# Values as weights and weighted transposition in the compressed-key attention layers of a four-layer transformer kernel

## What is computed

```
gates = sigmoid(g_logit)                       # one per head and branch
s_c = q . ck * scale - slope * dist_c ; p_cmp = masked_softmax(s_c)
o_cmp = p_cmp @ cv                             # 31 compressed keys
s_s = q . k_sel * scale - slope * dist ; o_sel = masked_softmax(s_s) @ v_sel
s_w = q . k_win * scale - slope * dist ; o_win = masked_softmax(s_w) @ v_win
out = g0 * o_cmp + g1 * o_sel + g2 * o_win
return out @ w_out
```

## Time and profile before

| | us |
|---|---|
| median of 3 runs | 2615.0 (2614.6 to 2615.92) |
| the profiled execution | 2615.86 |
| its span, first to last instruction | 2614.1 |
| TensorE busy | 2551.6 (98%) |
| VectorE busy | 1630.7 (62%) |
| ScalarE busy | 1171.1 (45%) |
| GpSimd busy | 359.3 (14%) |

### The profile page before, as it was taken

The page is one execution under the profiler, slowest core; times in us unless marked ns, Lnnn a source line. Parts: engine busy times, 40 slices in busy tenths (PEclk is TensorE's granted clock), DMA queues, the critical chain, the costliest instruction groups (busy, mean ns, idle before and its releaser), DMA issues.

```text
span 2614.1 us, 38319 instructions
## 1 busy us (share of the span) xinstructions
PE 2551.6 (98%) x13432; PEld 2152.9 (82%) x13432; DVE 1630.7 (62%) x2821; ACT 1171.1 (45%) x1799; POOL 359.3 (14%) x322
## 2 busy tenths in 40 slices
PE   8999999999999999999999999999999999999997
PEld 6999978888878677888878878888779998788886
DVE  6588667664252847667256676673386885766733
ACT  4367544443232845444235554443343774544421
POOL 2011121110010522111010021110010111211100
PEclk9999999999999999999999999999999999999999
DMA  4410023333233022332321123333333001233231
GB/s 156 142 33 1 26 81 97 96 96 98 81 109 97 17 65 89 97 96 90 106 79 62 41 81 103 96 97 97 94 113 105 9 2 49 89 97 97 88 105 48
DMA packets 61907, 210.90 MB, mean 81 GB/s; under 512 B 8528, under 2 KB 10320, under 8 KB 61776
## 3 DMA queue, kind: packets, MB, share of 16 engines
q1 hardware_dynamic: 61776, 209.13, 26.0%
HBM read 207.01 MB, written 2.10 MB: 80 GB/s over the span
## 4 chain that ended last, share of the span: by engine, by line
PE 90%; DVE 7%; ACT 1%; issue 1%; POOL 0%; DMA 0%; SPq 0%; DVEq 0%; ACTq 0%; POOLq 0%
PE psum L304 21%; PE psum L306 21%; PE psum L305 21%; PE psum L1077 6%; PE psum L1065 3%; PE psum L906 3%; PE psum L908 3%; PE psum L907 3%; PE psum L1055 2%; PE psum L1054 2%; DVE xl L477 2%; DVE h L494 2%; PE psum L338 1%; DVE dh L493 1%; PE psum L332 1%
## 5 line engine op out<-in xcount | busy, mean ns | idle before, releaser
L304 PE MATMUL psum<-xh,w_hi 128*128 128x512 f32 x1712 | 667.0, 390 | 0.1
L305 PE MATMUL psum<-xh,w_lo 128*128 128x512 f32 x1712 | 666.1, 389 | 0.0
L306 PE MATMUL psum<-xl,w_hi 128*128 128x512 f32 x1712 | 666.1, 389 | 0.0
L266 DVE TENSOR_TENSOR w_lo<-w_raw,w_hi 128x1024 fp32r<-128x1024 f32 x226 | 280.3, 1252 | 513.5 <-ACT w_hi L260 511.2
L260 ACT ACTIVATE w_hi<-w_raw 128x1024 fp32r<-128x1024 f32 x226 | 236.2, 1057 | 564.9 <-PE psum L306 455.1
L304 PEld LDWEIGHTS psum<-xh,w_hi 128*128 128x128 f32 x1712 | 321.4, 188 | 66.8 <-issue 0.6
L306 PEld LDWEIGHTS psum<-xl,w_hi 128*128 128x128 f32 x1712 | 321.3, 188 | 66.8
L305 PEld LDWEIGHTS psum<-xh,w_lo 128*128 128x128 f32 x1712 | 321.4, 188 | 66.4
L698 DVE TENSOR_TENSOR w_lo<-w_raw,w_hi 128x1024 fp32r<-128x1024 f32 x160 | 209.3, 1308 | 253.7 <-ACT w_hi L694 253.7
L304 PE MATMUL psum<-ah,w_hi 128*128 (+1 forms) x704 | 273.9, 389 | 0.0
L305 PE MATMUL psum<-ah,w_lo 128*128 (+1 forms) x704 | 273.9, 389 | 0.0
(11 more groups left out here) (198 smaller groups left out, 3837.4 us busy)
## 6 DMA issues: line engine op xcount, KB each, us to landing
w_raw<-w_up SPq DMA_DIRECT2D x176, 512.0 KB, 3.6
w_raw<-w_down SPq DMA_DIRECT2D x88, 512.0 KB, 3.6
w_raw<-nsa_in SPq DMA_DIRECT2D x56, 512.0 KB, 3.7
w_raw<-sb_in SPq DMA_DIRECT2D x24, 512.0 KB, 3.7
w_raw<-nsa_out SPq DMA_DIRECT2D x16, 512.0 KB, 3.7
w_raw<-swa_in SPq DMA_DIRECT2D x10, 512.0 KB, 3.7
w_raw<-sb_out SPq DMA_DIRECT2D x8, 512.0 KB, 3.7
w_raw<-swa_out SPq DMA_DIRECT2D x8, 512.0 KB, 3.7
```

The source lines that it names most:

```text
L266: nc.vector.tensor_tensor(w_lo[:, u % RING, :], w_raw[:, u % RING, :], w_hi[:, u % RING, :].bitcast(F32), ALU.subtract).then_inc(split_don ...
L304: nc.tensor.matmul(bank(p, o), wh[:, k, o, :], xhi(k), start=(first and k == 0), stop=False)
L305: nc.tensor.matmul(bank(p, o), wl[:, k, o, :], xhi(k), start=False, stop=False)
L306: mm = nc.tensor.matmul(bank(p, o), wh[:, k, o, :], xlo(k), start=False, stop=(last and k == 1))
```

## The change

In the two compressed-key layers the attention is written anew (`pe_steps`, `dve_steps`, `act_steps`, `pool_steps`); the sliding-window layer keeps the old functions. The unit is a step: two heads (a = 0, 1) and one query block, 16 steps per group, 64 per layer, in the order group, branch b, pair of heads p, i = 3, 2, 1, 0.

- Row sums come from the exponentials (`accum_out` into `rsums`). GpSimd takes the maximum with 1e-30 (`floor`), VectorE the reciprocal (`weights`), GpSimd multiplies it with the gate and the result with the identity: a tile with a head's factors on its diagonal (`scaled`).
- `transposes` is a float32 product of the raw exponentials as weights with that tile, so that transposed scores come out divided and gated.
- `copy` takes two PSUM banks to `pt`, ScalarE one and VectorE the other: for i = 3 and 2 a head each, for i = 1 ScalarE takes both heads, for i = 0 VectorE.
- `values` has 64 columns of values as weights and 128 queries moving, the two heads in the two halves of the columns. Both branches and the compressed branch add up in PSUM: one product of 512 columns with the compressed values (`cvb`) opens each pair. `mixed`, `output`, GpSimd's additions, `ot` and the 32 output transpositions fall away in these layers; the result is already turned, and ScalarE and VectorE make its high and low part from PSUM (`output`, `low`), mostly during the attention.
- Order: the scores of step t + 3 stand ahead of the transposing products of step t, and the values of t - 1 behind them.

```diff
-            for g in range(G):
-                shares = (pt[:, i, :] if i < 2 else late_pt[:, i - 2, :])[:, g * P:(g + 1) * P]
-                mm = nc.tensor.matmul(mix_bank(p0, i, g // 2)[:, 256 * (g % 2):256 * (g % 2) + 256], shares,
-                                      cvb[:, g, :], start=True, stop=True, skip_group_check=True)
...
+        def pe_steps(pe, l, last_unit):
...
+            def transposes(t):
+                it, b, p, i = step_of(t)
+                pe.wait_ge(nd_done, B + t + 1)
+                if t:
+                    pe.wait_ge(nca_done, C3 + act_copies(t - 1))
+                    pe.wait_ge(ncd_done, C3 + dve_copies(t - 1))
+                for a in range(2):
+                    x, at_ = turned_at(t, a)
+                    for j in range(i + 1):
+                        mm = nc.tensor.matmul(psum[:, half_of(l, 4 + x), at_ + j * P:at_ + (j + 1) * P], raw_scores(t, a)[:, j * P:(j + 1) * P],
+                                              scaled_unit(t)[:, a, :], start=True, stop=True, skip_group_check=True)
+                    mm.then_inc(nt_done, 1)
+            def values(t):
+                it, b, p, i = step_of(t)
+                o = half_of(l, 6 + p)
+                if b == 0 and i == TC - 1:
...
+                    nc.tensor.matmul(psum[:, o, :], cvb[:, it, P * p:P * p + P], ct[:, it, :], start=True, stop=False, skip_group_check=True)
...
+                for j in range(i + 1):
+                    for a in range(2):
+                        x, at_ = turned_at(t, a)
+                        mm = nc.tensor.matmul(psum[DH * a:DH * a + DH, o, i * P:(i + 1) * P], vt[b][:, j, it, 0:DH],
+                                              pt[:, 2 * (t % 2) + x, at_ + j * P:at_ + (j + 1) * P], start=False, stop=(b == 1 and j == i),
+                                              skip_group_check=True)
...
+            last_unit(ahead)
+            scores(2)
+            for t in range(STEPS):
+                if t + 3 < STEPS:
+                    scores(t + 3)
+                transposes(t)
+                if t:
+                    values(t - 1)
+            values(STEPS - 1)
+        def act_steps(act, l, window_values):
...
+            def exps(t):
+                n = (step_of(t)[3] + 1) * P
+                for a in range(2):
+                    c = 2 * (t % 4) + a
+                    v = raw_scores(t, a)[:, 0:n]
+                    act.wait_ge(nb_done, 2 * (B + t) + a + 1)
+                    nc.scalar.activation(v, v, ACT.Exp, scale=-1.0, bias=mins[:, c:c + 1], accum_out=rsums[:, c:c + 1]).then_inc(ne_done, 1)
+            def copy(t):
+                i = step_of(t)[3]
+                n = (i + 1) * P if i >= 2 else 2 * (i + 1) * P
+                act.wait_ge(nt_done, 2 * (B + t) + (1 if i >= 2 else 2))
+                if t >= 2:
+                    act.wait_ge(nv_done, B + t - 1)
+                nc.scalar.activation(pt[:, 2 * (t % 2), 0:n], psum[:, half_of(l, 4), 0:n], ACT.Copy).then_inc(nca_done, 1)
...
+            for t in range(STEPS):
+                it, x = t // 16, t % 16
+                if step_of(t)[3]:
+                    copy(t)
+                if t + 2 < STEPS:
+                    exps(t + 2)
...
+        def dve_steps(dve, ch, l, window_keys):
...
+            for t in range(STEPS):
+                it, x = t // 16, t % 16
+                if t + 1 < STEPS:
+                    weights(t + 1)
+                if step_of(t)[3] != 1:
+                    copy(t)
+                if t + 3 < STEPS:
+                    biased(t + 3)
...
+        def pool_steps(pool, l):
...
+            def floor(t):
+                c = 2 * (t % 4)
+                pool.wait_ge(ne_done, 2 * (B + t) + 2)
+                nc.gpsimd.tensor_scalar(rsums[:, 8 + c:10 + c], rsums[:, c:c + 2], 1e-30, None, ALU.max).then_inc(nf_done, 1)
+            def scaled(t):
+                it, b, p, i = step_of(t)
+                c, x = 2 * (t % 4), 3 * (R * it + 2 * p) + 1 + b
+                pool.wait_ge(nw_done, B + t + 1)
+                nc.gpsimd.tensor_tensor(rsums[:, 24 + c:26 + c], rsums[:, 16 + c:18 + c], gat[:, i, x:x + 4:3], ALU.mult).then_inc(ng_done, 1)
+                if t >= 4:
+                    pool.wait_ge(nt_done, 2 * (B + t - 4) + 2)
+                pool.wait_ge(ng_done, B + t + 1)
+                nc.gpsimd.tensor_tensor(scaled_unit(t), ident[:].unsqueeze(1).to_broadcast([P, 2, P]),
+                                        rsums[:, 24 + c:26 + c].unsqueeze(2).to_broadcast([P, 2, P]), ALU.mult).then_inc(nd_done, 1)
...
+            floor(0)
+            for t in range(STEPS):
+                if t + 1 < STEPS:
+                    floor(t + 1)
+                scaled(t)
...
```

More of the change, by code:

```diff
@@ L1146, in output @@
                         sums = bk[:, :, DH:DH + 1].rearrange("p t o -> p (t o)")
[L1147 to L1151, removed]
+                        dve.wait_ge(es_done, it * (n // 4) + (job + 1))
+                        mark[0] = ch.then(nc.vector.tensor_tensor(rs, sums, esink[:, job % 2, :], ALU.add))
                     if 1 in steps:
@@ L1186, in turn @@
                         output(job, (2,))
[L1187 to L1195, removed]
+                    r = s // 4 + 2
+                    if s % 4 == 1 and (more or r < R):
+                        queries(it + r // R, r % R)
                 if not more:
@@ L1218, in ahead @@
                     biased(0, s)
[L1219 to L1224, removed]
+            heads_loop(dve, ahead, turn, late)
         def act_attention(act, l, kind, late=None):
@@ L1260, in turn @@
                     exps(s)
-                    if kind == "nsa" and it == 0 and s == 1:
-                        late()
                     if 1 <= s % 4 <= 2:
                         copy(s - 1)
[L1265 to L1279, removed]
+                    r = s // 4 + 2
+                    if s % 4 == 0 and (more or r < R):
+                        queries(it + r // R, r % R)
             def ahead():
-                for r in range(R if kind == "nsa" else 2):
-                    queries(0, r)
-            heads_loop(act, ahead, turn, late if kind == "swa" else None)
+                queries(0, 0)
+                queries(0, 1)
+            heads_loop(act, ahead, turn, late)
         def slope(head):
@@ L1292, in esink_bias @@
             return sinks[:, bass.ds(it * R + r, 1)]
[L1294 to L1304, removed]
[L1305 to L1314 removed]
+        STEPS = 4 * H
@@ L1554, in exps @@
                 nc.scalar.activation(v, v, ACT.Exp, scale=-1.0).then_inc(ce_done, 1)
-            def mixed(i):
-                act.wait_ge(co_done, TC * k + i + 1)
-                for q in range(2):
-                    m = ch.then(nc.scalar.activation(ot[:, i, 512 * q:512 * q + 512], mix_bank(p0, i, q), ACT.Copy))
-                act.wait_ge(s_chain, m)
-                act.sem_inc(co_ready, 1)
             exps(0)
```

272 lines of the change are left out of this document (185 added, 87 removed).

## The result

| | before | after |
|---|---|---|
| median of the runs shown, us | 2615.46 (4 runs) | 2816.49 (4 runs) |
| lowest to highest, us | 2614.6 to 2615.99 | 2815.16 to 2817.88 |
| profiled execution, us (span, clock) | 2615.86 (2614.1, 0.997) | 2815.16 (2813.4, 0.975) |

The ratio is 1.0769, 95% interval 1.075 to 1.0788: slower, by 201 us. The forecast was 2734 us with a range up to 2780: right in sign, 82 us short, and outside the range.

The account below looks back on a forecast made before the run. TensorE bounds the kernel before; afterwards a ring of waits through ScalarE and GpSimd makes a pair 13.08 us against 8.97, +59.3 per layer. Two layers add 118.6 to 2615.9: 2734 us, range 2687 to 2780.

Parts of the forecast that it names:

- TensorE's own work: Compressed-key attention: TensorE alone needs 10.76 us per pair of heads in one branch, against 8.97 before.
- rival 2: Attention stage: TensorE decides, not the wait between engines; 10.76 us per pair, 2660 us; chance 0.10.
- The ring: Attention steps: products, copy, exponentials, floor, gate, scaled identity wait in a circle; 3.71 us in i = 3, 4.15 in i = 1.
- Value passes: Value products on TensorE: 0.055 us per pass, plus 0.15 per change of array form; 3.4 us per pair against 4.2.
- a transposing pass: Transposing fp32 products on TensorE: two passes each at 0.11 us, 4.4 us per pair, 2.2 more than before.
- rival 4: Transposing products: a true fp32 product costs four times a transposition; 17.0 us per pair, 2859 us; chance 0.02.
- Rival 1: GpSimd's scaled-identity tail slows by 1.4 beside VectorE; 14.03 us per pair, 2765 us; chance 0.12.
- granted clock of 1.00: TensorE in the attention stages: 2.4 GHz as in the earlier trace; a fall would lengthen the time, no size given.
- upper bound of 2778: Whole kernel, with small GpSimd operations at 0.41 us and sums at 0.08 per exponential: 14.43 us per pair.
- the tail: GpSimd's floor, gate and scaled identity with hand-overs, behind the exponentials: 1.15 us per step.
- read of ScalarE's accumulator: ScalarE delivering sums with exponentials: 0.04 us each, 0.08 in a step; bounds 0 and 0.08 per exponential.
- changes of form for free: TensorE's array-form switches without drain cost: 0.6 us per pair falls away, time about 2715 us.

Follow-up runs that it names:

- e8: e1 plus ScalarE's exponentials of two steps on issued ahead of the copy of the step's transposed half: 2671.12 us.
- e1: Changed kernel with GpSimd forming a step's scaled identity ahead of the next step's floor, not behind it: 2692.63 us.
- e2: Changed kernel, order kept, with 16 extra overwritten score products ahead of the real ones of each i=1 step: 2779.56 us.
- e9: e2 with the exponentials' sums left out, GpSimd taking score minima instead and the output's division omitted: 2752.94 us.
- e7: e8 with the exponentials and scaled identity written as float32r, so transposing products are not fp32 products: 2599.26 us.

## Why the prediction was right in sign and 82 us short

**Right.** TensorE's own work: 10.76 us per pair was forecast, and e8, where nothing else bounds, took 174.3 us for the stage, (174.3 + 3) / 16 = 11.1. As a time of the whole this is what rival 2 says, 2660 us; e8 measured 2671. The ring was right too, in its place and its members: the wait of 1.94 us before i = 0 (forecast about 2), 0.60 before i = 2 (forecast 0.5), none before i = 3 and i = 1 that mattered, the floor waiting for the exponentials; and e1, which only breaks that order, took it away. Value passes: 16 in 1.09 us with the group behind them 1.02 on, as forecast from the earlier trace rows; a transposing pass 0.11, as read from the earlier trace rows, so rival 4 is out. Rival 1 is out too: the scaled identity took 0.61 us in all 128 cases, with VectorE at work beside it (at 259.12) and without (at 267.34). Outside the stages 7 us were given back, 7 forecast; 1.2 of them come from the start, where nothing was forecast.

**Wrong, first: the clock.** The step that failed is the one sentence under "How the numbers follow": the granted clock of 1.00 was carried over from the earlier trace rows, a stage without a gap, to a stage into which the same text put a gap of 1.8 us 16 times. That it would then be "longer still" was said, but given neither a price nor a place in the range. Its price by e2 is 37 us (2816.5 to 2779.6): in the half-clock stretches a transposing pass takes about 0.2 us, twice the 0.11 of the rows. An estimate from the stretches alone: 27 of them (two follow the last wait of a stage, of 1.73 us) last 117 us together in the trace after, so they lose at most half of that, 58 us. Put on the forecast of 2734, such a term gives 2792 us, still short of the measured time; put on the upper bound of 2778 it would have held it. The Trainium skill, TensorE: Matmul & The Clock Gate, Part 1, says that the halved clock is the default state and that activity releases it. e2 agrees: with activity in the wait the clock stays up.

**Wrong, second: the ring's small terms.** e2 has the ring at full clock: 2779.6 us, 45 over the forecast. By steps, from the first transposing product of one to that of the next, in the period of e2 from 250.71 to 264.97 us, which has no compressed values; the last row is what is missing to the mean of 14 periods, 14.46 us:

| step | forecast | measured | what was mis-sized |
|---|---|---|---|
| i = 3 | 3.71 | 4.09 | ring |
| i = 2 | 3.21 | 3.60 | ring, which was to lie under TensorE's own 3.21 |
| i = 1 | 4.15 | 4.58 | ring |
| i = 0 | 1.58 | 1.99 | products start anew behind a wait, the scaled identity of i = 3 is ready late |
| compressed values, mean | 0.43 | 0.20 | partly in the shadow of the ring |

Together 1.38 us per pair, times 32 some 44 of the 45 us. In the rows of the i = 1 step above the 0.43 divides so: the eight passes and the way to the copy 1.19 (263.43 to 264.62) against 1.08; the exponentials with their reads 1.51 (265.12 to 266.63) against 1.42; the tail behind them 1.38 (266.63 to 268.01) against 1.15. GpSimd's three operations were well sized, 0.21 + 0.20 + 0.61 against 0.18 + 0.18 + 0.64; their hand-overs were not: 0.08 + 0.08 + 0.14 + 0.06 where 0.15 stood for all. The read of ScalarE's accumulator had no row before and was put at 0.04 per exponential by VectorE's 0.08; it is an instruction of 0.19 with some 0.1 of its own on ScalarE when an exponential follows, and all of it counts when GpSimd waits. By e9 the reads cost 0.83 per pair; 0.24 was charged. The upper bound, 0.08 per read, was taken from another engine's row, and was no bound.

One sum in the prediction is off as well. With changes of form for free it takes 0.6 us per pair off the forecast and gets 2715 us. The 0.6 holds only beside its bound with GpSimd's small operations at nothing. With its own 3.16 for the ring of i = 2 the step goes from 3.21 to 3.16 only, and what falls away is some 0.5 us, 2719 us.

**Where the time went**, from before to after: TensorE's own new work 55 us (e8); ScalarE's copy ahead of the exponentials 21.5 (e8 to e1); the ring 87 (e1 to e2); the clock 37 (e2 to after). The sum is 201. These are steps along one path; the second pass, 72 us by e7 against e8, lies in the first of them, so without it TensorE's new work would have been a gain of 17.

## What to carry to other kernels

A floor of two numbers on an engine that is 16% busy can set the period of the kernel: for each engine write down which instruction stands ahead of the one that is waited for, and what that one waits for. When a forecast puts a wait on TensorE, price the clock with it, from the granted clock that the passes behind the wait would have; a wait that can't be removed may be worth filling with work that is thrown away. And before weighting inside a transposition, ask for the format: in fp32 the weighting costs a second pass, in float32r none.

## What the runs showed of the hardware

- A wait of 1.9 us, once in 15.6, was followed in 25 of 30 cases by a granted clock of 0.5 for 3.4 or 6.8 us, starting between 0.3 us before and 2.3 us after TensorE was at work again. With waits of 0.5 us alone in the steady part (e1) the clock stayed at 1.00 throughout the stage.
- ScalarE's sum output is an instruction of its own, 0.19 us; it delays the next exponential by about 0.1 and a waiting engine by all of it.
- GpSimd takes 0.20 to 0.21 us for a 128x2 operation, and 0.06 to 0.14 us lie between the end of an operation and the start of one that waits for it, on GpSimd or on its way from ScalarE and to TensorE. Its 128x256 product took 0.61 us whether VectorE worked beside it or not.
- An fp32 product of 128x128 is two instructions of 0.11 us, a float32r one is a single instruction of 0.11 to 0.12, like an fp32 transpose.
